# Turning P*V round in the attention of a two-layer fp32 decoder trunk, with the softmax denominators spread by TensorE

## What is computed

```
# sliding window, in blocks of 128 queries
s = q @ k.T * scale ; masked
m = max(max(s), sink) ; p = exp(s - m)
denom = sum(p) + exp(sink - m)
out = (p / denom) @ v            # per head, then concatenated
y = out @ w_out

# forgetting attention
s = q @ k.T * scale + c_t - c_s ; causal
out = softmax(s) @ v ; y = out @ w_out
```

## Time and profile before

| | |
|---|---|
| runs | 2195.68, 2193.16, 2195.62 us; median 2195.62 |
| profiled execution | 2193.65 us, span 2192.0 us |
| PE busy | 2168.5 us, 99% |
| DVE busy | 1373.1 us, 63% |
| ACT busy | 1139.3 us, 52% |
| granted TensorE clock | 0.999 of full speed (mean), that is its upper level, 2.4 GHz |

### The profile page before, as it was taken

The page is one execution under the profiler, slowest core; times in us unless marked ns, Lnnn a source line. Parts: engine busy times, 40 slices in busy tenths (PEclk is TensorE's granted clock), DMA queues, the critical chain, the costliest instruction groups (busy, mean ns, idle before and its releaser), DMA issues.

```text
span 2192.0 us, 32365 instructions
## 1 busy us (share of the span) xinstructions
PE 2168.5 (99%) x10193; PEld 1787.9 (82%) x10193; DVE 1373.1 (63%) x2436; ACT 1139.3 (52%) x2061; POOL 107.5 (5%) x215
## 2 busy tenths in 40 slices
PE   8999999999999999999999999999999999999998
PEld 6887888888888888887888887888888888888886
DVE  7677576655666655567675666566655666655665
ACT  7645565444444444455655545564544454545452
POOL 2000000000000000000130230000000000000000
PEclk9999999999999999999999999999999999999999
DMA  8543666656666656665655654656566666566652
GB/s 262 165 123 102 216 195 189 192 182 191 191 198 185 186 187 191 196 193 153 205 151 173 183 163 144 209 188 199 184 190 201 191 191 191 175 190 203 195 184 88
DMA packets 205034, 399.85 MB, mean 182 GB/s; under 512 B 12720, under 2 KB 12880, under 8 KB 204448
## 3 DMA queue, kind: packets, MB, share of 16 engines
q1 hardware_dynamic: 202496, 390.12, 57.2%
q0 software_dynamic: 2320, 8.72, 1.3%
q10 hardware_dynamic: 144, 0.07, 0.0%
HBM read 396.72 MB, written 2.13 MB: 182 GB/s over the span
## 4 chain that ended last, share of the span: by engine, by line
PE 95%; DVE 2%; issue 1%; ACT 1%; DMA 1%; POOL 0%; POOLq 0%; DVEq 0%; ACTq 0%; SPq 0%
PE bank L1082 30%; PE bank L1084 30%; PE bank L1083 30%; PE bank L1133 1%; PE bank L1170 1%; PE bank L1144 1%; PE bank L1157 1%; PE bank L1095 1%; PE bank L1159 1%; PE bank L1158 1%; PE bank L1111 1%; DMA stage<-swa_w_in 0%; PE bank L1119 0%; DVE ring_lo L642 0%; DVE prob L718 0%
## 5 line engine op out<-in xcount | busy, mean ns | idle before, releaser
L1082 PE MATMUL bank<-ring_hi,a_hi 128*128 128x512 f32 x2240 | 886.1, 396 | 0.9 <-DVE ring_lo L642 0.9
L1084 PE MATMUL bank<-ring_hi,a_lo 128*128 128x512 f32 x2240 | 874.0, 390 | 0.0
L1083 PE MATMUL bank<-ring_lo,a_hi 128*128 128x512 f32 x2240 | 872.6, 390 | 0.0
L456 ACT ACTIVATE ring_hi<-stage,g_t 128x512 fp32r<-128x512 f32 x992 | 662.8, 718 | 370.7 <-PE bank L1084 221.5
L642 DVE SCALAR_TENSOR_TENSOR ring_lo<-stage,g_t,ring_hi 128x512 fp32r<-128x512 f32 x992 | 701.7, 753 | 199.4 <-ACT ring_hi L456 198.5
L1084 PEld LDWEIGHTS bank<-ring_hi,a_lo 128*128 128x128 f32 x2240 | 420.8, 188 | 89.4
L1082 PEld LDWEIGHTS bank<-ring_hi,a_hi 128*128 128x128 f32 x2240 | 421.1, 188 | 87.3 <-issue 2.9
L1083 PEld LDWEIGHTS bank<-ring_lo,a_hi 128*128 128x128 f32 x2240 | 421.4, 188 | 83.0
L640 DVE TENSOR_TENSOR ring_lo<-stage,ring_hi 128x512 fp32r<-128x512 f32 x480 | 304.5, 686 | 162.8 <-ACT ring_hi L454 162.7
L454 ACT ACTIVATE ring_hi<-stage 128x512 fp32r<-128x512 f32 x480 | 271.9, 623 | 164.4 <-PE bank L1084 150.8
L1082 PE MATMUL bank<-ring_hi,h_hi 128*128 128x512 f32 x704 | 276.6, 393 | 0.0
(11 more groups left out here) (134 smaller groups left out, 955.9 us busy)
## 6 DMA issues: line engine op xcount, KB each, us to landing
stage<-ffn_w_gate_up SPq DMA_DIRECT2D x352, 512.0 KB, 3.7
stage<-ffn_w_down SPq DMA_DIRECT2D x176, 512.0 KB, 5.7
stage<-fox_w_in SPq DMA_DIRECT2D x96, 512.0 KB, 4.1
stage<-swa_w_in SPq DMA_DIRECT2D x48, 512.0 KB, 4.4
stage<-swa_w_out SPq DMA_DIRECT2D x32, 512.0 KB, 3.3
stage<-fox_w_out SPq DMA_DIRECT2D x32, 512.0 KB, 5.2
g_b<-norm_gains POOLq DMA_DIRECT2D x4, 1024.0 KB, 7.0
cum_b<-cum_scratch POOLq DMA_DIRECT2D x32, 128.0 KB, 3.5
```

The lines of the kernel that those rows point to most:

```text
L456: nc.scalar.activation(ring_hi[:, n % RING, :], src, ACT.Identity, scale=g_t[:, row * KT + j:row * KT + j + 1]).then_inc(hi_ready, 1)
L1082: nc.tensor.matmul(dst, hi_a, hi_w, start=start, stop=False)
L1083: nc.tensor.matmul(dst, hi_a, lo_w, start=False, stop=False)
L1084: return nc.tensor.matmul(dst, lo_a, hi_w, start=False, stop=stop)
```

## The change

P*V is turned round: V is the stationary operand (64 columns) and the transposed P the moving one (256 columns with the first block of keys, 128 with the second). The two heads of a pair go to the two column halves of the array, partitions 0 to 63 and 64 to 127 of `o_ps`, so o comes out already transposed. The denominators then have to lie along the free dimension: VectorE's reciprocal reads `den` with each value repeated 64 times and writes 128x512 into `rden_w`; TensorE transposes that (`spread_denominators`, in the place of `transpose_o`), ScalarE copies it from `tr_ps` to the place of o in `o_t` (`read_spread`, in the place of VectorE's `read_output`), and VectorE multiplies it by `o_ps` in place (`divide_output`, in the place of `normalise`). The next P*V into the bank waits for `divided`. VectorE's reciprocal comes one pair earlier in its program, the division one step after the P*V. The steps `o0`, `o1` and that of the first transposes of q or k (`qk0`) move. The order of heads in `o_t` changes (`head_slot`), and with it the order of rows in which the output weights of the sliding layer are loaded: two transfers of 64 partitions for one of 128. POOL's load of gains waits for the last P*V instead of the last transposes.

```diff
-STD = dict(tr=4, first=6, every=4, o0=21, o1=29)
-LAST = dict(tr=2, first=3, every=3, o0=14, o1=21)
+STD = dict(tr=4, first=6, every=4, o0=18, qk0=21, o1=26)
+LAST = dict(tr=2, first=3, every=3, o0=12, o1=18)
...
-                return w.rearrange("(a h p) n -> h p a n", a=2, h=2)[half]
+                return [w[row:row + PAIR * DH].rearrange("(m d) n -> d m n", d=DH)
+                        for row in (PAIR * DH * half, CH // 2 + PAIR * DH * half)]
...
-            return 4 * (m // 2) + (2 * a + m % 2 if G < NG else 2 * (m % 2) + a)
+            return 2 * m + a
...
-            if holds_qk(u) and s == (28 if u == U_FOX else 24):
+            if holds_qk(u) and s == (28 if u == U_FOX else 24 if attended(u) is None else STD["qk0"]):
...
-                    sp.dma_start(stage[:, slot * PAIR:(slot + 1) * PAIR, :], weights(u, i, pr)).then_inc(raw_loaded[slot], 16)
+                    to = stage[:, slot * PAIR:(slot + 1) * PAIR, :]
+                    if U_SWA_OUT <= u < U_FFN[0]:
+                        for a, rows in enumerate(weights(u, i, pr)):
+                            sp.dma_start(to[DH * a:DH * (a + 1)], rows).then_inc(raw_loaded[slot], 16)
+                    else:
+                        sp.dma_start(to, weights(u, i, pr)).then_inc(raw_loaded[slot], 16)
...
+            def read_spread(G, i, g4):
+
+                act.wait_ge(tr_done, TR[("o", G, g4)] + 1 + TR_LOOP * i)
+                first = 4 * (G % NG) + 2 * g4 + 4 * i
+                nc.scalar.activation(o_t[:, bass.ds(first, 2), :], tr_ps[:, :].rearrange("p (k m) -> p k m", k=2),
+                                     ACT.Identity).then_inc(tr_read, 1)
...
                         m = pair_step(when, s, 0)
                         if m is not None:
                             exponentials(G, i, m, 0)
+                        if s in (when["o0"], when["o1"]):
+                            read_spread(G, i, (when["o0"], when["o1"]).index(s))
...
-            def read_output(G, i, g4):
-                n = TR[("o", G, g4)]
-                dve.wait_ge(tr_done, n + 1 + TR_LOOP * i)
+            def divide_output(G, i, g4):
+
+                dve.wait_ge(tr_read, TR[("o", G, g4)] + 1 + TR_LOOP * i)
+                dve.wait_ge(pv_done, 2 * G + g4 + 1 + 2 * i)
                 first = 4 * (G % NG) + 2 * g4 + 4 * i
-                nc.vector.tensor_copy(o_t[:, bass.ds(first, 2), :], tr_ps[:, :].rearrange("p (k m) -> p k m", k=2)).then_inc(tr_read, 1)
+                o = o_t[:, bass.ds(first, 2), :]
+                nc.vector.tensor_tensor(o, o_ps[:, :].rearrange("p (k m) -> p k m", k=2), o, ALU.mult).then_inc(divided, 1)
...
-                    nc.vector.reciprocal(rden[:, part, :], den[:, part, :]).then_inc(den_inverted, 1)
+                    nc.vector.reciprocal(wide, den[:, part, :].rearrange("p j t -> p t j").unsqueeze(3).to_broadcast([P, NT, 4, DH])).then_inc(den_inverted, 1)
...
                         m = pair_step(when, s, 2)
+                        if m in (0, 2):
+                            denominators(G, i, m // 2)
+                        m = pair_step(when, s - 1, 2)
                         if m in (1, 3):
-                            denominators(G, i, m // 2)
-                            normalise(G, i, m // 2)
-                        if s == when["o0"]:
-                            read_output(G, i, 0)
-                        if s == when["o1"]:
-                            read_output(G, i, 1)
+                            divide_output(G, i, m // 2)
...
-                pool.wait_ge(tr_done, TR[("o", NG * layer + NG - 1, 1)] + 1)
+                pool.wait_ge(pv_done, 2 * NG * (layer + 1))
...
-            def transpose_o(G, i, g4):
-                pe.wait_ge(o_normed, 2 * G + g4 + 1 + 2 * i)
+            def spread_denominators(G, i, g4):
+
+                pe.wait_ge(den_inverted, 2 * G + g4 + 1 + 2 * i)
                 free_tr(TR[("o", G, g4)], i)
                 for k in range(2):
                     for t in range(NT):
-                        last = nc.tensor.transpose(tr_ps[:, (2 * k + t) * P:(2 * k + t + 1) * P], o_sb[:, t, k * P:(k + 1) * P], ident[:, :])
+                        last = nc.tensor.transpose(tr_ps[:, (2 * k + t) * P:(2 * k + t + 1) * P], rden_w[:, t, k * P:(k + 1) * P], ident[:, :])
...
             def times_v(G, i, m):
-                dst = o_ps[:, :].rearrange("p (t j d) -> p t j d", t=NT, d=DH)
-                for a in range(2):
-                    n = GH * G + 2 * m + a
-                    pe.wait_ge(pt_read, n + 1 + GH * i)
-                    if m % 2 == 0 and a == 0 and n > 0:
-                        pe.wait_ge(o_normed, n // 4 + 2 * i)
-                    v0 = DH * (2 * G + a) if G < NG else DH * (2 * m + a)
-                    j = head_slot(G, m, a) % 4
-                    pt = prob_t[:, a, :]
-                    nc.tensor.matmul(dst[:, 0, j], pt[:, 0:P], v_sb[:, 0, v0:v0 + DH], start=True, stop=True)
-                    nc.tensor.matmul(dst[:, 1, j], pt[:, P:2 * P], v_sb[:, 0, v0:v0 + DH], start=True, stop=False)
-                    last = nc.tensor.matmul(dst[:, 1, j], pt[:, 2 * P:3 * P], v_sb[:, 1, v0:v0 + DH], start=False, stop=True)
+                n = GH * G + 2 * m
+                if m % 2 == 0 and n > 0:
+                    pe.wait_ge(divided, n // 4 + 2 * i)
+                for part, (lo, hi) in enumerate(((0, 2 * P), (2 * P, 3 * P))):
+                    for a in range(2):
+                        if part == 0:
+                            pe.wait_ge(pt_read, n + a + 1 + GH * i)
+                        v0 = DH * (2 * G + a) if G < NG else DH * (2 * m + a)
+                        dst = o_ps[DH * a:DH * (a + 1), SEQ * (m % 2) + P * part:SEQ * (m % 2 + 1)]
+                        last = nc.tensor.matmul(dst, v_sb[:, part, v0:v0 + DH], prob_t[:, a, lo:hi], start=part == 0, stop=part == 1)
```

More of the change, by code:

```diff
@@ L241, in build @@
         pt_done, pt_read, pv_done = sem("pt_done"), sem("pt_read"), sem("pv_done")
-        sink_diff, sink_exp, den_added, den_inverted, o_normed = (sem(n) for n in ("sink_diff", "sink_exp", "den_added", "den_inverted", "o_normed"))
+        sink_diff, sink_exp, den_added, den_inverted = (sem(n) for n in ("sink_diff", "sink_exp", "den_added", "den_inverted"))
+        divided = sem("divided")
         ot_hi = [sem(f"ot_hi{t}") for t in range(NT)]
@@ L286, in weights, with loads_before @@
             return cols(fox_w_out[0], CH * (u - U_FOX_OUT))
+        def loads_before(pair):
+            turn = pair // NSTAGE + 1
+            in_halves = min(max(turn - U_SWA_OUT * UT // STAGE, 0), NC_D * UT // STAGE)
+            return 16 * (turn + in_halves)
         def gain_row(u):
@@ L447, in round_tile @@
                 if j % PAIR == 0:
-                    act.wait_ge(raw_loaded[pair % NSTAGE], 16 * (pair // NSTAGE + 1) + 16 * LT // STAGE * i)
+                    act.wait_ge(raw_loaded[pair % NSTAGE], loads_before(pair) + 16 * LT // STAGE * i)
                 if n >= RING:
@@ L516, in sink_terms @@
                                          ACT.Exp).then_inc(sink_exp, 1)
+            def read_spread(G, i, g4):
[3 more added lines that the diff above has]
+                                     ACT.Identity).then_inc(tr_read, 1)
             def o_heads(layer, kp, t):
                 G, g4 = divmod(kp, 2)
-                act.wait_ge(tr_read, TR[("o", NG * layer + G, g4)] + 1)
+                act.wait_ge(divided, 2 * (NG * layer + G) + g4 + 1)
                 wait_swept(act, (U_SWA_OUT, U_FOX_OUT)[layer] - 1, 0, t)
@@ L740, in denominators @@
                 dve.wait_ge(exped, GH * G + 4 * g4 + 4 + GH * i)
+                if n > 0:
+                    before = ("o", G, 0) if g4 else ("o", G - 1, 1) if G < NG else ("qk", U_FOX + 3 * (G - NG) + 2, 0)
+                    dve.wait_ge(tr_done, TR[before] + 1 + TR_LOOP * i)
+                wide = rden_w[:, :, :].rearrange("p t (j d) -> p t j d", d=DH)
                 if G < NG:
@@ L744, in denominators @@
                     dve.wait_ge(den_added, n + 1)
-                    nc.vector.reciprocal(rden[:, part, :], den_all[:, part, :]).then_inc(den_inverted, 1)
+                    nc.vector.reciprocal(wide, den_all[:, part, :].rearrange("p j t -> p t j").unsqueeze(3).to_broadcast([P, NT, 4, DH])).then_inc(den_inverted, 1)
                 else:
-                    nc.vector.reciprocal(rden[:, part, :], den[:, part, :]).then_inc(den_inverted, 1)
[L749 to L759, removed]
+                    nc.vector.reciprocal(wide, den[:, part, :].rearrange("p j t -> p t j").unsqueeze(3).to_broadcast([P, NT, 4, DH])).then_inc(den_inverted, 1)
             def o_rests(layer, kp, t):
@@ L951, in _ @@
             dve.wait_ge(sinks_loaded, 16)
-            for a in range(2):
-                last = nc.vector.tensor_copy(sinks_p[:, :].rearrange("p (g h a b) -> p a g h b", g=NG, h=2, a=2)[:, a],
-                                             sinks[:, :].rearrange("p (g a h b) -> p a g h b", g=NG, a=2, h=2)[:, a])
```

(3 more changed lines are left out.)

11 lines of the change are left out of this document (5 added, 6 removed).

## The result

The changed kernel takes 2199.61 us (median of 17 runs, 2197.98 to 2201.55); the kernel before took 2193.99 us beside it (17 runs, 2192.59 to 2197.23). The ratio is 1.0023 with a 95% interval of 1.0016 to 1.0031, so it is slower by 5.6 us. The profiled execution took 2200.21 us with a span of 2198.6 us, against 2193.65 and 2192.0 before.

What follows compares the result with a forecast made beforehand. TensorE, busy 99% of the span, was taken as the bound. Six normal groups -10.3 saved and +10.1 in waits, last groups +5.9 net, sum to +5.7 us: 2200 us, range 2182 to 2210.

Steps and rivals of the forecast that it cites:

- The bound: TensorE, busy 99% of the span: time taken off it is gained unless something new makes it wait.
- P*V: Turned-round P*V on TensorE saves 0.53 us behind scores, 0.33 alone; 1.72 a group, 13.8 over eight groups.
- The halves side by side: P*V's two column halves overlap as the scores' do: 0.66 us a pair streaming, against 1.3 otherwise.
- rival 2: P*V's column halves run one behind the other, 0.65 us more on 32 pairs: +12 us, 2207; chance 0.16.
- The reciprocal: VectorE's reciprocal of 512 elements a partition is paid by the element and takes 3.2 us.
- rival 1: The reciprocal streams elements as fast as other operations, 0.73 us: -12 us, 2184; chance 0.22.
- Rival 3: The reciprocal takes 3.7 us or more; at 4.1 us the change costs +20 us, 2215; chance 0.12.
- Waits in normal groups: TensorE waits for VectorE 1.0 and 0.45 us a group, 1.3 and 0.6 with sinks; +10.1 us over six groups.
- The last groups: Each layer's last group, a pair every 3 steps, loses net +2.9 us, +3.0 with sinks; +5.9 together.
- The third wait of 1.1, at the second spread: In a last group the second reciprocal ends 1.1 us after TensorE has come to its spread.
- The base: +5.7 us gives 2199.4 on the profiled 2193.65, 2201.3 on the median of 2195.62; 2200 taken.
- The rest priced at nothing: Split output-weight transfers, ScalarE's 16 reads except as counted, and POOL's changed wait: no cost.

Runs made afterwards that it cites:

- short_reciprocal: The changed kernel, but VectorE inverts only the 8 denominators and a second VectorE copy widens them to 512 columns; 2180.67 us, ratio 0.9936 to the kernel before.
- half_long: short_reciprocal, but for the first 128 tokens the reciprocal itself writes the widened 256 columns; 2185.39 us, ratio 0.9958 to the kernel before.
- one_half: The changed kernel with both heads of a pair on the lower column half, one after the other; 2205.13 us, ratio 1.0048 to the kernel before.
- sizes: The kernel before, plus unused reciprocals of 1 to 128 elements a partition and copies of 1 to 128 at VectorE's start; 2196.11 us, one run.
- read_first: The changed kernel with ScalarE's read of the spread ahead of the next pair's first exponentials; 2199.55 us, ratio 1.0022 to the kernel before.
- before_plus_wide_reciprocal: The kernel before, plus one unused 512-column VectorE reciprocal for each two pairs; 2218.51 us, ratio 1.0109 to the kernel before.

## Why the prediction was right

2200 us were predicted and 2199.61 measured, and the sign held: slower, by a gain on TensorE and a larger loss through VectorE. Step by step:

- **The bound.** Right. Where VectorE had room again (the normal groups of short_reciprocal, those of the forgetting layer in half_long) all that P*V gave back arrived at the end.
- **P*V.** Saved 1.72 us a group in the forecast, 1.87 measured. Behind the scores the saving is 0.54, predicted 0.53 (a step with scores, P*V and transposes went from 3.00 to 2.46 us by the distance of its neighbours); the term mis-sized is P*V without scores, 0.40 and not 0.33. Over eight groups 15.0 in place of 13.8 us. PE's busy time fell by 9 us and not by 14: part of it, some 3 us, is the work at the lower clock in the last groups; I didn't trace the rest.
- **The halves side by side.** Right, and rival 2 is out: one_half is that rival built, at +5.5 us on the change and not +7: 4.9 in the normal groups, where the rival had 5.5, and 0.5 in the last ones, where it had 1.1. "TensorE: Matmul & The Clock Gate" of the Trainium skill, Part 3 (The mechanism), says that a load overlaps a running matmul only where row groups differ. Here two column halves that share all 128 rows ran with starts 7 ns apart, the upper half's load (1205.240) behind the start of the lower half's matmul (1205.235), so for column halves the trace decides against the reading that I took from it.
- **The reciprocal.** 3.2 us taken, 3.34 to 3.35 measured; by the element, 6.25 ns, in the 5.5 to 6.8 worked out from two small rows. That the number came so close is in good part luck: sizes shows that 8 elements don't lie on the line yet. There the reciprocal of 8 takes 171 ns and a copy of 8 takes 163; by the same working these two would have given some 2 ns an element and 1.2 us, on the side of rival 1. The choice of a cost by the element was right, its size wasn't to be had from such rows. Rival 1 fell with it: its kernel would have been one that takes no more than short_reciprocal, and that is what 0.7 us are worth, -13 us against the -12 forecast. Rival 3's 4.1 us isn't reached. The Trainium skill's "VectorE: DVE Perf Modes" (the fixed hardware budget) names a repeat count of 8 for the iterative divide; the eight cycles an element that I read into it would be an estimate of 4.4 us, and the measured 6.25 ns are six at the page's 0.96 GHz.
- **Waits in normal groups.** The forgetting layer's: 1.0 and 0.45 us forecast. Against the same steps of short_reciprocal, which hold no wait, the group shown loses 0.70 (transposes of k) + 0.34 (P*V of pair 2) + 0.62 (second spread) = 1.66 us; the three groups lose 1.65, 1.65 and 1.24. The chain was the one written out, up to who reads the spread behind whose exponential; read_first shows that it doesn't matter which of the two places holds the wait. With sinks 2.12, 2.15 and 2.49 against 1.9. So the six groups paid 11.3 us where the sum had 10.1, and got back 11.6 where it had 10.3: two terms too small by about as much, in opposite directions.
- **The last groups.** The balance held, +3.25 and +3.29 us against +3.0 and +2.9, but one term of it didn't. Counted from the first main product of the unit, P*V of pair 2 comes at 22.10 us before and at 24.50 after in the forgetting layer: 2.4 late, forecast 2.5. The third wait of 1.1, at the second spread, is not there. In its place the products at the lower clock kept TensorE about 1.6 us longer on its way, and it came to the spread at 1381.40, when the reciprocal of 1378.00 had just ended (1381.34). In read_first the clock stays up in this layer, and there the wait is, 1.16 us before that spread; the unit takes 39.59 us against 40.09, that is +2.8 on the kernel before, the forecast's +2.9 nearly to the letter. So the fall cost 1.6 us and hid 1.1, and the sum came out right partly because of that: nothing in the forecast had a fall of the clock.
- **The base.** The sum was 2199.4 beside the profiled execution and 2201.3 beside the median of three; 17 runs put the median before at 2193.99, near the first, and 2193.99 + 5.7 is 2199.7.

The rest priced at nothing stayed there: the three units of the sliding layer's output projection behind the last group, whose weights come by the two transfers, take 21.76, 21.76 and 23.63 us in both kernels.

## What to carry to other kernels

Price a special function of VectorE by the element, from two sizes at least, and not from the smallest (up to 8 elements the time here hardly moved): what is nothing at 8 elements (0.2 us) can be 3.3 us at 512. Do such an operation on the narrow data and widen the result with a copy (0.2 + 0.5 us here), on whichever engine isn't late. And before moving work from the bounding engine to one that is 78% busy beside it, count that engine's room in the very stretch: here 2.13 us a half group were free in the forgetting layer, and of what 3.34 us had above that more than half came back as waits of the bounding engine.

## What the hardware showed that was not expected

**The granted clock fell behind long waits of TensorE, but not behind all of them.** In the changed kernel both last groups show 0.50 (the lower level) for five or six main products, after waits of 1.8 and 2.3 us in the one and 1.6 and 1.9 in the other. In before_plus_wide_reciprocal it is 8.1 and 7.7 us after a single wait of 4.45, and in the first layer of read_first at least the 2.9 us shown, after one of 1.79:

```profile
212.20:215.10 2.90, 2.90 (x8) 2.27 (x7) 2.80 (x14) 2.46 (x9) 0.00 (x0) 0.50 0.00 0
```

In the second layer of read_first waits of 1.59 and 1.87 us, and in one_half waits of 0.93 and 2.26 and of 1.13 and 1.85, left it at 1.00. The length of the wait alone doesn't decide: at the start of the forgetting layer TensorE waits 1.97 us in short_reciprocal, and the clock falls, and 1.98 us in half_long, where it doesn't; the unit takes 27.92 us in the one and 26.35 in the other. The kernel before waits 2.31 us there and keeps 1.00. What else it takes is open; nothing was run to bring the fall about by itself.

**Column halves share the array as well as row halves**: eight 64-column records in 0.81 us side by side, 1.44 one behind the other.
